# The end of a two-layer mixer and expert kernel: last scatter by halves, squares behind each addition, the usual path straight on, stores from two queues

## What is computed

```python
for l in range(DEPTH):
    h = rmsnorm(x, attn_norm_g[l])
    x = x + hybrid_mixer(h, ...)
    h = rmsnorm(x, ffn_norm_g[l])
    if l % 2 == 0:
        x = x + swiglu(h, ffn_w_gate[j], ffn_w_up[j], ffn_w_down[j])
    else:
        x = x + moe_swiglu(h, router_w[j], router_b[j], moe_w_gate[j], moe_w_up[j], moe_w_down[j])
return rmsnorm(x, final_norm_g)
```

## Time and profile before

| what | value |
|---|---|
| median of 3 runs | 1564.58 us (1563.92 to 1565.61) |
| the profiled execution's own time | 1564.46 us |
| its span | 1562.8 us |
| TensorE (PE) busy | 1521.1 us, 97% |
| VectorE (DVE) busy | 1231.1 us, 79% |
| ScalarE (ACT) busy | 945.8 us, 61% |
| GpSimd (POOL) busy | 34.6 us, 2% |
| DMA, mean | 263 GB/s |
| TensorE's granted clock, mean | 0.991 |
| chain that ended last | PE 92%, DVE 4%, ACT 2%, issue 1%, DMA 1% |

### The profile page before, as it was taken

The page is one execution under the profiler, slowest core; times in us unless marked ns, Lnnn a source line. Parts: engine busy times, 40 slices in busy tenths (PEclk is TensorE's granted clock), DMA queues, the critical chain, the costliest instruction groups (busy, mean ns, idle before and its releaser), DMA issues.

```text
span 1562.8 us, 19329 instructions
## 1 busy us (share of the span) xinstructions
PE 1521.1 (97%) x7552; PEld 1272.0 (81%) x7552; DVE 1231.1 (79%) x1214; ACT 945.8 (61%) x872; POOL 34.6 (2%) x66
## 2 busy tenths in 40 slices
PE   6999999999999999999899999999999999999995
PEld 5898888888887898888688888888888888888884
DVE  5679876654547688866798998989989899899995
ACT  5346534544444356634677777777777777777774
POOL 2000000000000000000100000000000000000000
PEclk9999999999999999999899999999999999999997
DMA  7444445454555444544999998999989999899960
GB/s 272 178 154 172 179 168 189 171 190 184 192 185 185 175 182 153 194 161 152 373 366 375 357 367 327 360 377 353 368 325 351 386 352 369 319 363 378 353 251 29
DMA packets 113938, 411.66 MB, mean 263 GB/s; under 512 B 13168, under 2 KB 13216, under 8 KB 113840
## 3 DMA queue, kind: packets, MB, share of 16 engines
q1 hardware_dynamic: 111152, 401.73, 69.1%
q0 software_dynamic: 2688, 8.61, 1.7%
HBM read 409.24 MB, written 1.05 MB: 263 GB/s over the span
## 4 chain that ended last, share of the span: by engine, by line
PE 92%; DVE 4%; ACT 2%; issue 1%; DMA 1%; SPq 0%; DVEq 0%; ACTq 0%
PE ps L988 31%; PE ps L621 20%; PE ps L999 14%; PE ps L889 8%; PE ps L611 4%; PE ps L903 4%; PE ps L600 3%; DVE w_lo L1510 1%; PE ps L949 1%; PE ps L1016 1%; PE ps L958 1%; DVE w_lo L1373 1%; ACT w_hi L1063 1%; DMA raw_m<-dense_dram 1%; PE ps L579 1%
## 5 line engine op out<-in xcount | busy, mean ns | idle before, releaser
L1510 DVE TENSOR_TENSOR w_lo<-late,w_hi 128x2048 fp32r<-128x2048 f32 x192 | 438.0, 2289 | 39.7 <-ACT w_hi L1123 39.7
L1123 ACT CAST w_hi<-late 128x2048 fp32r<-128x2048 f32 x192 | 367.3, 1913 | 41.7 <-PE ps L988 41.7
L1373 DVE TENSOR_TENSOR w_lo<-raw_m,w_hi 128x2048 fp32r<-128x2048 f32 x117 | 267.3, 2290 | 141.4 <-ACT w_hi L1063 141.0
L1063 ACT CAST w_hi<-raw_m 128x2048 fp32r<-128x2048 f32 x117 | 222.0, 1906 | 142.7 <-PE ps L621 67.8
L988 PE MATMUL ps<-w_hi,hT_hi 128*128 128x512 f32 x704 | 281.8, 400 | 2.9 <-DVE w_lo L1510 2.9
L988 PE MATMUL ps<-w_hi,hT_lo 128*128 128x512 f32 x704 | 274.8, 390 | 0.0
L988 PE MATMUL ps<-w_lo,hT_hi 128*128 128x512 f32 x704 | 274.7, 390 | 0.0
L621 PE MATMUL ps<-w_hi,hT_hi 128*128 128x512 f32 x480 | 190.7, 397 | 2.1 <-DVE w_lo L1373 1.2
L621 PE MATMUL ps<-w_hi,hT_lo 128*128 128x512 f32 x480 | 187.7, 391 | 0.0
L621 PE MATMUL ps<-w_lo,hT_hi 128*128 128x512 f32 x480 | 187.7, 391 | 0.0
L1510 DVE TENSOR_TENSOR w_lo<-raw_m,w_hi 128x2048 fp32r<-128x2048 f32 x72 | 165.0, 2292 | 24.6 <-ACT w_hi L1123 24.6
(11 more groups left out here) (332 smaller groups left out, 2100.9 us busy)
## 6 DMA issues: line engine op xcount, KB each, us to landing
late<-experts_dram SPq DMA_DIRECT2D x384, 512.0 KB, 4.9
raw_m<-dense_dram SPq DMA_DIRECT2D x234, 512.0 KB, 4.0
raw_m<-experts_dram SPq DMA_DIRECT2D x144, 512.0 KB, 4.8
bias<-b_in_dram POOLq DMA_DIRECT2D x26, 256.0 KB, 4.6
xt<-x_dram SPq DMA_DIRECT2D x4, 256.0 KB, 5.6
out_dram<-xn SPq DMA_DIRECT2D x4, 256.0 KB, 2.5
tmp<-w_small_dram POOLq DMA_DIRECT2D x2, 320.0 KB, 4.0
tmp<-ffn_norm_g_dram POOLq DMA_DIRECT2D x1, 512.0 KB, 3.9
```

The lines of the kernel that those rows point to most:

```text
L1063: copy(w_hi[:, g % RS, :], slot_raw(g, False)).then_inc(hi_ready, 1)
L1123: copy(w_hi[:, m % RS, :], slot_raw(m, True)).then_inc(hi_ready, 1)
L1373: tt(w_lo[:, g % RS, :], slot_raw(g, False), w_hi[:, g % RS, :], ALU.subtract)\
L1510: tt(w_lo[:, m % RS, :], slot_raw(m, True), w_hi[:, m % RS, :], ALU.subtract).then_inc(lo_ready, 1)
```

## The change

- *Scatter* (TensorE, last expert): half 0 of both tiles, then half 1 of both tiles; half 0 waits for half 0 of `ysb` alone. Banks 6, 7, 0, 1, one for each product. VectorE's additions go in the same order.
- *Transposes* (TensorE): those for the last block of the last expert stand between the two halves of `dn 9`.
- *Squares* (ScalarE): each waits for its addition instead of for a piece of `xn`, and the table load stands ahead of the branch.
- *Products with the gain*: GpSimd makes half 0 of both tiles behind the half 0 additions, VectorE half 1 of both.
- *Branches*: VectorE and ScalarE load the count in expert 3, at `dn 6`. The condition is turned round: `final(0)` stands in the `If`, `moe_pass(1)` and `final(1)` in the `Else`. GpSimd has such a branch too. TensorE's and SyncE's stay as they were.
- *Norm*: the five small steps become four (two fused ones in place of three), at all five calls.
- *Scaling and stores*: VectorE scales three pieces and SyncE stores them, ScalarE scales tile 1's half 0 and issues its store itself.

The diff, cut to its core (not shown: a renamed semaphore, and the old text of the moved transposes):

```diff
@@ -147,9 +147,9 @@
...
-        for t in range(2):
-            fills((pas, E - 1), f"sc{t}", (6, 7))
-
+        for h, t, b in ((0, 0, 6), (0, 1, 7), (1, 0, 0), (1, 1, 1)):
+            FILL[(pas, E - 1), f"sc{t}", h] = (b, nfill[b])
+            nfill[b] += 1
@@ -448,11 +448,10 @@
...
-            for h in range(2):
-                for t in range(NT):
-                    sp.wait_ge(scaled[t], h + 1)
-                    sp.dma_start(out[t * P:(t + 1) * P, h * W:(h + 1) * W], xn[:, t, h * W:(h + 1) * W])\
-                        .then_inc(out_done, 16)
+            for n, (t, h) in enumerate(((0, 0), (0, 1), (1, 1))):
+                sp.wait_ge(scaled, n + 1)
+                sp.dma_start(out[t * P:(t + 1) * P, h * W:(h + 1) * W], xn[:, t, h * W:(h + 1) * W])\
+                    .then_inc(out_done, 16)
             sp.wait_ge(out_done, 32 * NT)
@@ -547,6 +546,21 @@
...
+            def first_rows(pas):
+
+                for t in range(NT):
+                    b, k = FILL[(pas, E - 1), f"sc{t}", 0]
+                    pool.wait_ge(drained[b], k + 1)
+                    nc.gpsimd.tensor_tensor(xn[:, t, 0:W], xt[:, t, 0:W], fin_g[:, 0:W], ALU.mult)\
+                        .then_inc(final_rows, 1)
+
+            pool.wait_ge(pos_ready, 1)
+            many = pool.value_load(cnt_i[0:1, 0:1], min_val=0, max_val=T)
+            with pool.If(many <= P):
+                first_rows(0)
+            with pool.Else():
+                first_rows(1)
@@ -965,6 +979,15 @@
...
+            def rows_hidden_T(l, x, i):
+
+                await_drained(l, f"gu{i}")
+                b = claim(l, f"hT{i}")
+                for m in range(2):
+                    ins = nc.tensor.transpose(ps[:, b, m * P:(m + 1) * P], hid[:, (i + x) % 2, m * P:(m + 1) * P],
+                                              ident[:, :])
+                done(ins, l, f"hT{i}")
@@ -1002,6 +1025,8 @@
...
                             if i == NF - 1:
                                 done(ins, l, "acc", h)
+                            if h == 0 and (e, i) == (E - 1, NF - 2):
+                                rows_hidden_T(l, x, NF - 1)
                     if USED[MOE_BASE + pas * NM + m][0] == "w":
                         ins.then_inc(w_used, 1)
...
                     ih = next_hidden(kind, i, c)
...
+                    if ih is not None and (e, ih) != (E - 1, NF - 1):
+                        rows_hidden_T(l, x, ih)
...
-                rows_out(pas, E - 1)
...
+                l = pas, E - 1
+                await_drained(l, "selT")
+                for h in range(2):
+                    await_drained(l, "acc", h)
+                    for t in range(NT):
+                        b = claim(l, f"sc{t}", h)
+                        for y in (ysb_hi, ysb_lo):
+                            ins = mm(ps[:, b, :], selT((E - 1) % 2)[:, t, :], y[:, 4 * h:4 * h + 4, :],
+                                     start=(y is ysb_hi), stop=(y is ysb_lo))
+                        done(ins, l, f"sc{t}", h)
@@ -1298,8 +1325,12 @@
...
                     l, x = (pas, e), e % 2
+                    if pas == 0 and (e, kind, i) == (3, "dn", 6):
+                        act.wait_ge(pos_ready, 1)
+                        many = act.value_load(cnt_i[0:1, 0:1], min_val=0, max_val=T)
@@ -1319,23 +1350,31 @@
...
-            moe_pass(0)
-            many = act.value_load(cnt_i[0:1, 0:1], min_val=0, max_val=T)
-            with act.If(many > P):
+                return many
+
+            def final(pas):
+
+                for h in range(2):
+                    for t in range(NT):
+                        await_drained((pas, E - 1), f"sc{t}", h)
+                        scratch = ytok[:, h, :] if t == 0 else tmp[:, h * W:(h + 1) * W]
+                        A(scratch, xt[:, t, h * W:(h + 1) * W], ACT.Square, accum_out=(ss, ss1)[h][:, t:t + 1])\
+                            .then_inc(stat, 1)
+                norm_stats()
+                act.wait_ge(rfin_ready, 1)
+                act.wait_ge(final_rows, NT)
+                link(A(xn[:, 1, 0:W], xn[:, 1, 0:W], ACT.Copy, scale=rfin[:, 1:2]))
+                act.dma_start(out[P:2 * P, 0:W], xn[:, 1, 0:W]).then_inc(out_done, 16)
+
+            many = moe_pass(0)
+            load_sqrt()
+            counts = seq[0], norms[0]
+            with act.If(many <= P):
+                final(0)
+            seq[0], norms[0] = counts
+            with act.Else():
                 moe_pass(1)
-            load_sqrt()
-            for h in range(2):
-                for t in range(NT):
-                    act.wait_ge(final_rows, NT * h + t + 1)
-                    scratch = ytok[:, h, :] if t == 0 else tmp[:, h * W:(h + 1) * W]
-                    A(scratch, xt[:, t, h * W:(h + 1) * W], ACT.Square, accum_out=(ss, ss1)[h][:, t:t + 1])\
-                        .then_inc(stat, 1)
-            norm_stats()
-            act.wait_ge(rfin_ready, 1)
-            for h in range(2):
-                c = slice(h * W, (h + 1) * W)
-                A(xn[:, 1, c], xn[:, 1, c], ACT.Copy, scale=rfin[:, 1:2]).then_inc(scaled[1], 1)
+                final(1)
@@ -1396,9 +1435,8 @@
...
                 link(tt(nt0, y0, y0, ALU.mult))
-                link(tt(nt0, nt0, var, ALU.mult))
-                link(ts(nt0, nt0, -0.5, 1.5, ALU.mult, ALU.add))
-                tt(r, y0, nt0, ALU.mult).then_inc(ready or rstd_ready, 1)
+                link(stt(nt0, nt0, -0.5, var, ALU.mult, ALU.mult))
+                stt(r, nt0, 1.5, y0, ALU.add, ALU.mult).then_inc(ready or rstd_ready, 1)
@@ -1847,11 +1885,15 @@
...
+            def add_half(pas, e, t, h):
+
+                b = await_full((pas, e), f"sc{t}", h)
+                r = xt[:, t, h * W:(h + 1) * W]
+                tt(r, r, ps[:, b, :], ALU.add).then_inc(drained[b], 1)
+
             def add_rows(pas, e, t):
                 for h in range(2):
-                    b = await_full((pas, e), f"sc{t}", h)
-                    r = xt[:, t, h * W:(h + 1) * W]
-                    tt(r, r, ps[:, b, :], ALU.add).then_inc(drained[b], 1)
+                    add_half(pas, e, t, h)
@@ -1864,8 +1906,11 @@
...
                     l, x = (pas, e), e % 2
+                    if pas == 0 and (e, kind, i) == (3, "dn", 6):
+                        many = dve.value_load(cnt_i[0:1, 0:1], min_val=0, max_val=T)
@@ -1907,25 +1952,32 @@
...
+                for h in range(2):
+                    for t in range(NT):
+                        add_half(pas, E - 1, t, h)
+                return many
+
+            def final(pas):
+
+                dve.wait_ge(fg_in, 48)
                 for t in range(NT):
-                    add_rows(pas, E - 1, t)
-                for t in range(NT):
-                    for h in range(2):
-                        await_drained((pas, E - 1), f"sc{t}", h)
-
-            moe_pass(0)
-            many = dve.value_load(cnt_i[0:1, 0:1], min_val=0, max_val=T)
-            with dve.If(many > P):
+                    await_drained((pas, E - 1), f"sc{t}", 1)
+                    note(tt(xn[:, t, W:D], xt[:, t, W:D], fin_g[:, W:D], ALU.mult))
+                norm(rfin, rfin_ready)
+                settle()
+                dve.wait_ge(final_rows, NT)
+                for t, h in ((0, 0), (0, 1), (1, 1)):
+                    c = slice(h * W, (h + 1) * W)
+                    ts(xn[:, t, c], xn[:, t, c], rfin[:, t:t + 1], None, ALU.mult).then_inc(scaled, 1)
+
+            many = moe_pass(0)
+            counts = seq[0], nnorm[0]
+            with dve.If(many <= P):
+                final(0)
+            seq[0], nnorm[0] = counts
+            with dve.Else():
                 moe_pass(1)
-            dve.wait_ge(fg_in, 48)
-            for h in range(2):
-                c = slice(h * W, (h + 1) * W)
-                for t in range(NT):
-                    tt(xn[:, t, c], xt[:, t, c], fin_g[:, c], ALU.mult).then_inc(final_rows, 1)
-            norm(rfin, rfin_ready)
-            for h in range(2):
-                c = slice(h * W, (h + 1) * W)
-                ts(xn[:, 0, c], xn[:, 0, c], rfin[:, 0:1], None, ALU.mult).then_inc(scaled[0], 1)
+                final(1)
```

13 lines of the change are left out of this document (3 added, 10 removed).

## The result

| | before | after |
|---|---|---|
| median of 5 runs | 1565.42 us (1563.92 to 1567.87) | 1557.44 us (1556.46 to 1558.06) |
| ratio of the medians, 95% interval | | 0.995 (0.9938 to 0.9961) |
| profiled execution / its span | 1564.46 / 1562.8 us | 1557.26 / 1555.5 us |
| TensorE's granted clock, mean | 0.991 | 0.995 |

What follows compares the result with a forecast made beforehand. TensorE is busy almost throughout up to the last expert; some 13 us of the tail are serial, a good half waiting. 0.40 + 2.21 + 5.06 + 0.20 + 0.20 = 8.07 us less than 1564.46 gives 1556.4, range 1554.6 to 1559.4.

Steps and rivals of the forecast that it cites:

- Transposes: Last hidden transposes moved between the halves of the block before: -0.40 us, bounds 0 and -1.1.
- Scatter by halves: Last expert's scatter starts on the first half alone, VectorE the bound; last addition done at 1546.76 instead of 1548.97: -2.21 us.
- From the last addition to the statistics' product: Tail before the norm: 2.23 us in place of 7.29, -5.06; bounds -5.97 and about -3.2.
- the hold: VectorE's pair of multiplications, possible from 1546.67, waits until GpSimd's two end at 1547.58.
- Rivals 1 and 2: 1: GpSimd doesn't hold VectorE, 1555.5 us, chance 0.22; 2: the fall-through path is fetched too, 1558.3 us, chance 0.13.
- One step less in the norm: One small step saved per norm: -0.20 us at the end, -0.20 at the router, 0 at the others.
- Early loads of the count: ScalarE and VectorE load the count in expert 3: cost 0, or 0.45 us if the cover is gone.
- Stores from two queues: ScalarE issues one store beside SyncE's three at the end: 0, bounds -0.45 and +0.3 us.
- S: The moment the scaling begins, forecast to move from 1557.75 to about 1549.7.
- 5.0 us from S to the end: Sign expected in the profile after: the time from the start of the scaling to the end is 5.0 us.
- rival 3: Exit jump over the second pass is late on ScalarE: 1.2 us later, 1557.6, up to 1558.0; chance 0.15.
- Rival 4: Exit jump's fetch starts among the stores and takes up to 17.8 us: 13.9 more, 1570.3 us; chance 0.03.

## Why the prediction was right, and where it was not

*Transposes* (-0.40): 0.41, from the run with them back. *Scatter by halves* (-2.21): 2.16, from the run with the halves alone. The two together are 2.57, and the changed kernel shows 2.58.

*From the last addition to the statistics' product* (-5.06): -5.21, the 0.15 more being the hold that cost less. The mechanism was as told. The squares are off the path, the branch that falls through costs nothing (its compare and branch took 0.05 us), and VectorE's first product is held until GpSimd's second is done. Rivals 1 and 2 are answered by it: the hold costs 0.75 here (2.04 against 1.29), not 0.91, since the pair began before GpSimd had finished and only the first of it was held. The Trainium skill's rule in SBUF — State Buffer, on who interferes with whom, holds with GpSimd first too, as these rows show it.

*One step less in the norm* (-0.20 twice): 0.21 at the end. At the router the changed kernel's chain has its steps at 755.02, 755.22, 755.42 and 755.61, one less, so 0.2 is right, but the 0.50 measured up to the hidden product can't be told from scatter: the same product starts between 1536.55 and 1538.21 in ten executions of kernels that share all code up to it, and at 1540.02 and 1540.83 in the two with the slow clock at 690. That this 0.30 offsets part of the stores' 1.21 is luck.

*Early loads of the count* (0): ScalarE's cast at 1122.20 stood 0.44 behind, as forecast, and from the first expert's selection to the last one's TensorE took 678.9 us in both kernels. Nothing is lost.

*Stores from two queues* (0, at most +0.3): this is **the step that failed**. I took S to the end as unchanged, because the DMA engines are full whoever issues. It became 1.21 longer in the profile, well over the +0.3 that I allowed, and 0.5 to 1.2 in the two profiled executions of this code, and of the signs I had named the "5.0 us from S to the end" failed with 6.26. The cause isn't the second queue but the exit jumps that the turned-round branches bring: their code fetches run beside the stores. I had seen that jump (rival 3) and asked only whether ScalarE would be late itself. It wasn't: its fetch took some 3.5 us and it drained at S + 4.76, ahead of the last store, which by my own test rules rival 3 out. That rival's price of 1.2 agrees with the measured 1.21 by chance. What I didn't ask is what the fetch does to the traffic beside it. The Trainium skill, in Runtime: NRT & Kernel Launch, on instruction fetch, says that a taken branch to a place outside two pages forces a DMA fetch before execution goes on. The runs agree (2.02 us ahead of the pair with the jump, none without), and that the fetch also slows others' transfers stands here only by the runs.

Rival 4, a fetch that is itself delayed by the stores up to 17.8 us, didn't happen: 3.5 in place of 2.7. The sum of the deviations, -0.30 + 0.03 - 0.15 - 0.01 + 1.21 + 0.10 = +0.88, is, but for rounding, the difference between 1556.39 and the profiled 1557.26. The stores' 1.21 is larger than it, so the 1556.4 came as close as it did because the parts ahead of S were better by 0.43.

Shown by the runs: that the lengthening goes with exit fetches inside the stores (five tails without, nine with, and no overlap), and that in the changed kernel it is VectorE's and ScalarE's exit jumps that bring it: with these two gone and the other exits as they were the tail is 4.65, with TensorE's put off in their place it stays at 5.18. Not settled: why a small packet of code lengthens an issue of a store from 0.43 to 1.27 us, and why the same code has tails of 5.17 and 5.86.

## What to carry to other kernels

When a branch is turned round so that the usual path falls through, the jump doesn't vanish but moves to the path's end; look at what runs there, for its fetch costs its own time (2.0 to 3.5 us here) and can also slow transfers of other engines beside it. The better place for the jump is an idle stretch of the engine before the critical stretch: with the branch in VectorE's 2.71 us of waiting, no exit jump of VectorE and ScalarE and no product for GpSimd the kernel takes 1555.88 us (before 1564.36 beside it), the lowest median of all; against the changed kernel's 1556.96 beside it the ranges overlap, so five runs each don't prove that last step. And where GpSimd is given half of VectorE's work to save time, check whether both read SBUF twice: here VectorE waited for it, and making the product part of the scaling instead brought S 1.2 us forward.

## What was not expected of the hardware

- A store's issue on SyncE, 0.43 to 0.47 us undisturbed (the second and later ones), took up to 1.27 with a code fetch of another engine beside it; the second one took 0.68 to 1.27 in all nine such executions.
- A branch that isn't taken costs VectorE and ScalarE 0.04 to 0.05 us and no idle time behind it; one that is taken costs VectorE 2.0 to 2.8 us, and TensorE's compare and branch took 3.87 here and 5.05 before.
- With equal code ahead of it and no gap in its work, TensorE was granted a mean of 1.00, 0.83 or 0.66 in the same 10 us (690 to 700). Of the six runs of one kernel those with a mean clock of 0.991 to 0.992 took 1 to 6 us longer than those with 0.994 to 0.995.
